# A ring of eleven 2 MB weight blocks over the mixer's buffers, and 32 experts written out, in a one-layer decoder kernel in fp32

## The reference, cut to what matters

```python
h = rmsnorm(x, norm_mix_g)
x = x + hybrid_mixer(h, w_in, conv_w, w_gk_up, b_gk_up, gla_norm_g, w_out)
h = rmsnorm(x, norm_ffn_g)
x = x + moe(h, w_router, b_router, w_gate_up, b_gate_up, w_down, b_down)
out = rmsnorm(x, norm_final_g)

def moe(h, ...):
    top_v, top_i = lax.top_k(h @ w_router + b_router, 4)    # 32 logits for each token
    gates = softmax(top_v)
    # for each expert e, over the tokens that chose it:
    gu = xb @ w_gate_up[e] + b_gate_up[e]                   # 1024 -> 2048
    gate, up = min(gu[:, :F], 7), clip(gu[:, F:], -7, 7)
    y += gate_e * (((up + 1) * gate * sigmoid(1.702 * gate)) @ w_down[e] + b_down[e])   # 1024 -> 1024
```

## Time and profile before

| | |
|---|---|
| time, median of 3 runs | 1104.35 us (1102.31 to 1104.95) |
| the profiled execution's own time | 1101.66 us |
| its span in the trace | 1099.9 us |
| TensorE busy | 1021.7 us, 93% of the span |
| VectorE busy | 222.4 us, 20% |
| ScalarE busy | 163.9 us, 15% |
| read from HBM | 422.56 MB, 385 GB/s over the span |
| mean granted TensorE clock | 0.991 |

### The profile page before, as it was taken

One profiled execution on the slowest core, in us unless ns is written; L12 is line 12 of the kernel. 1 busy time (PEld: TensorE's weight loads), 2 busy tenths in 40 slices (PEclk: granted clock), 3 DMA queues, 4 the chain that ended last, 5 costly groups with the idle time before them and its releaser, 6 DMA issues.

```text
span 1099.9 us, 12562 instructions
## 1 busy us (share of the span) xinstructions
PE 1021.7 (93%) x4660; PEld 393.9 (36%) x4660; DVE 222.4 (20%) x621; ACT 163.9 (15%) x316; POOL 9.6 (1%) x25
## 2 busy tenths in 40 slices
PE   6999989999999999999999999999999999999995
PEld 5588553333333323333333333333332333233331
DVE  1253141111111111111111111111111111111113
ACT  2211021111111111111111111111111111111112
POOL 2000000000000000000000000000000000000000
PEclk9999979999999999999999999999999999999998
DMA  9823338999999999999999999999999999999994
GB/s 375 320 86 144 105 153 343 430 428 429 429 429 429 429 428 428 428 427 429 428 428 428 428 427 429 429 429 428 428 429 429 429 429 428 428 428 427 429 428 170
DMA packets 31337, 423.77 MB, mean 385 GB/s; under 512 B 4623, under 2 KB 4798, under 8 KB 5694
## 3 DMA queue, kind: packets, MB, share of 16 engines
q1 hardware_dynamic: 29454, 421.57, 90.8%
q10 hardware_dynamic: 1872, 2.05, 0.7%
HBM read 422.56 MB, written 1.05 MB: 385 GB/s over the span
## 4 chain that ended last, share of the span: by engine, by line
DMA 59%; PE 38%; DVE 1%; issue 1%; ACT 1%; SPq 0%; ACTq 0%; PEldq 0%; DVEq 0%
DMA ring<-in_w_down 58%; PE bank L1129 13%; PE bank L1116 8%; PE bank L916 6%; PE bank L1005 3%; PE bank L1145 2%; PE bank L912 1%; PE bank L1070 1%; PE bank L1178 1%; DMA x_sb<-in_x 0%; PE bank L1024 0%; PE bank L904 0%; PE bank L1078 0%; DVE y_out L875 0%; PE bank L977 0%
## 5 line engine op out<-in xcount | busy, mean ns | idle before, releaser
L1116 PE MATMUL bank<-ring,x_t 128*64 128x512 f32 x2048 | 466.4, 598 | 13.5 <-DMA ring<-in_w_gate_up 12.5
L1129 PE MATMUL bank<-ring,act 128*64 128x512 f32 x1024 | 239.0, 598 | 32.3 <-DMA ring<-in_w_down 32.3
L1116 PEld LDWEIGHTS bank<-ring,x_t 128*64 128x64 f32 x2048 | 134.0, 136 | 295.7 <-issue 244.1
L1129 PEld LDWEIGHTS bank<-ring,act 128*64 128x64 f32 x1024 | 68.5, 136 | 173.8 <-issue 117.7
L824 DVE TENSOR_TENSOR gu_b<-bank,bias_e 128x512 f32<-128x512 f32 x64 | 44.2, 691 | 350.8 <-PE bank L1145 350.8
L768 DVE TENSOR_SCALAR p_row<-slot,rank 128x64 f32 (+1 forms) x64 | 13.3, 252 | 394.4 <-issue 394.3
L533 ACT COPY gu_sb<-bank 128x512 f32<-128x512 f32 x64 | 37.4, 585 | 244.0 <-PE bank L1116 244.0
L916 PE MATMUL bank<-h_t,ring 128*128 128x256 f32 x320 | 70.3, 380 | 1.3 <-ACT h_t L425 1.3
L1178 PE MATMUL bank<-z,p_t 64*128 64x512 f32 x256 | 63.6, 615 | 0.7 <-ACT z L549 0.7
L916 PEld LDWEIGHTS bank<-h_t,ring 128*128 128x128 f32 x320 | 60.4, 190 | 10.0 <-ACT h_t L425 1.5
L1070 PE MATMUL bank<-h,p_row 128*64 128x512 f32 x256 | 62.2, 607 | 0.0
(11 more groups left out here) (184 smaller groups left out, 334.5 us busy)
## 6 DMA issues: line engine op xcount, KB each, us to landing
ring<-in_w_gate_up SPq DMA_DIRECT2D x128, 2048.0 KB, 24.0
ring<-in_w_down SPq DMA_DIRECT2D x64, 2048.0 KB, 24.4
ring<-in_w_in SPq DMA_DIRECT2D x6, 2048.0 KB, 20.2
ring<-in_w_out SPq DMA_DIRECT2D x2, 2048.0 KB, 11.7
x_sb<-in_x SPq DMA_DIRECT2D x2, 512.0 KB, 4.1
out<-y_out SPq DMA_DIRECT2D x2, 512.0 KB, 2.7
gffn_bc<-in_norm_ffn_g ACTq DMA_DIRECT2D x1, 512.0 KB, 11.0
g_bc<-in_norm_final_g ACTq DMA_DIRECT2D x1, 512.0 KB, 26.3
```

Source lines behind the costliest of these rows:

```text
L1116: ins = mm(bank[h][a * SLOTS:(a + 1) * SLOTS, :], x_t[:, k, :], w[:, kk, a, :], start=k == 0, stop=k == KT - 1)
L1129: ins = mm(bank[0][a * SLOTS:(a + 1) * SLOTS, :], act[:, k, :], w[:, kk, a, :], start=k == 0, stop=k == KT - 1)
```

## The change

- `ring` has eleven slots of 2 MB in place of six. All SBUF tensors get addresses by hand. Slots 6 to 10 lie over the mixer's temporaries (`slot_at(6)` to `slot_at(10)`), so each can be loaded for an expert only when the mixer has done with what lies there.
- SP's first eleven expert loads wait for different things: four for mixer chunks as before, number 4 for the decays and the turned k, 5 to 7 for the attention's and convolution's outputs, 8 and 9 for the two `w_out` chunks, 10 for the gates; from number 11 on a load waits for the use of the chunk that is eleven before it.
- The 32 experts are written out on PE, ACT, DVE and SP, with no loop; further items, where there are any, run one by one in a loop of their own behind them (`If(n > E)`).
- `h2` is gone: `p_row` holds the norm factor in place of ones, the gather takes x itself, and the norm's weights are multiplied in when DVE (no longer ACT) keeps the turned rows as `x_t` (`keep_turned`).
- The first gather stands ahead of the sums for the table; the table's sums and the `b_down` products (now four of fp32 with 32 rows each, no split copy) stand in item 0, behind its first chunk (`start_sums`).
- Small parameters come in one array of columns (`cols_in`), `w_router` and `b_gate_up` are laid out on the host as they are used, so two small turns and the sixteen of L1043 go. `b_gate_up` and `b_down` are loaded early on ACT's queue; `norm_final_g` at the end, on SP's queue, into a slot that is free by then.

The core of the diff:

```diff
-RING = 6
+RING = 11
+MIX_SLOTS = 6
+ORDER = (2, 3, 4, 5, 6, 7, 8, 9, 0, 1, 10)
+LOADED_BEFORE = (2, 2, 1, 1, 1, 1, 0, 0, 0, 0, 0)
+LAST = (E - 1) * ITEM_CHUNKS
...
+def expert_slot(it, j):
+    g = it * ITEM_CHUNKS + j if isinstance(it, int) else LAST + j
+    return ORDER[g % RING]
...
+        ring = [at(f"ring{i}", [P, CHUNK], slot_at(i)) for i in range(RING)]
...
 @block.sync
-            with sp.Fori(0, E) as it:
-                load_item(it, it)
+            for it in range(E):
+                for j in range(ITEM_CHUNKS):
+                    g = it * ITEM_CHUNKS + j
+                    if g < 4:
+                        sp.wait_ge(s_used, 2 + g + 1)
+                    elif g == 4:
+                        sp.wait_ge(s_dec, 4)
+                        sp.wait_ge(s_ex, 3)
+                        sp.wait_ge(s_kt, 1)
+                    elif g == 5:
+                        sp.wait_ge(s_o, 2)
+                        sp.wait_ge(s_ms, 2)
+                        sp.wait_ge(s_ygla, 2)
+                    elif g == 6:
+                        sp.wait_ge(s_o, 2)
+                    elif g == 7:
+                        sp.wait_ge(s_ygla, 2)
+                        sp.wait_ge(s_yconv, 2)
+                    elif g < 10:
+                        sp.wait_ge(s_used, MIX_CHUNKS)
+                    elif g == 10:
+                        sp.wait_ge(s_gtk, 1)
+                    else:
+                        sp.wait_ge(s_used, MIX_CHUNKS + g - RING + 1)
+                    load(it, j, it)
...
 @block.vector
-                dve.scalar_tensor_tensor(out=h2[:, t, :], in0=xs[:, t, :], scalar=rstd[:, t:t + 1],
-                                         in1=gffn_bc[:, :], op0=ALU.mult, op1=ALU.mult).then_inc(s_h2, 1)
...
-                    dve.tensor_scalar(p_row[:, t, :], s1[:, ds(boff, SLOTS)], rank1[:, t, ds(e, 1)], None, ALU.is_equal)
+                    dve.tensor_scalar(p_row[:, t, :], slots, rank1[:, t, ds(e, 1)], rstd[:, t:t + 1],
+                                      ALU.is_equal, ALU.mult)
...
+            def keep_turned(it):
+                dve.wait_ge(s_xT, it + 1)
+                g = cols[:, COL_FFN:COL_FFN + KT].rearrange("p (a f s) -> p a f s", a=2, s=1)
+                dve.tensor_tensor(x_t[:, :, :].rearrange("p (a f) s -> p a f s", a=2),
+                                  bank[3][:, :].rearrange("p (f a s) -> p a f s", f=4, a=2),
+                                  g.broadcast_to([P, 2, 4, SLOTS]), ALU.mult).then_inc(s_xt, 1)
...
 @block.tensor
+            def start_sums():
+                pe.wait_ge(s_hot, 1)
+                for a in range(2):
+                    for b in range(nb):
+                        ins = mm(bank[7][0:1, 128 + a * EXTRA:128 + (a + 1) * EXTRA],
+                                 exp_c[:, 0:1] if a == 0 else boff_c[:, b:b + 1], hot[:, b, :],
+                                 start=b == 0, stop=b == nb - 1)
+                ins.then_inc(s_tab, 1)
+                pe.wait_ge(s_gtk, 3)
+                pe.wait_ge(s_bias, 16 * (1 + SPLITS))
+                pe.wait_ge(s_table, 1)
+                for t in range(TT):
+                    for nn in range(2):
+                        i = 2 * t + nn
+                        ins = mm(y_ps[t][nn][:, :], gates_t[i * E:(i + 1) * E, t, :], bdn[i * E:(i + 1) * E, :],
+                                 start=True, stop=True, tile_position=(i * E, 0))
+                ins.then_inc(s_mixed, 1)
...
-            with pe.Fori(0, final) as it:
-                products(it, last=False)
-            products(final, last=True)
+            for it in range(E):
+                if it == 2:
+                    pe.wait_ge(s_items, 1)
+                    n = pe.value_load(n_items[0:1, 0:1], min_val=E, max_val=E + EXTRA)
+                products(it, it + 1 if it + 1 < E else None)
+            with pe.If(n > E):
+                with pe.Fori(E, n) as it:
+                    pe.wait_ge(s_p, it + 1)
+                    pe.wait_ge(s_ptk, it)
+                    gather()
+                    turn_gathered(it)
+                    products(it, None)
```

More of the change, by code:

```diff
@@ L44, with mix_slot, expert_loaded, build @@
 HALF = 512
[L47 to L52, removed]
+ORDER = (2, 3, 4, 5, 6, 7, 8, 9, 0, 1, 10)
+LOADED_BEFORE = (2, 2, 1, 1, 1, 1, 0, 0, 0, 0, 0)
+LAST = (E - 1) * ITEM_CHUNKS
+SPARE = [ORDER[(LAST + ITEM_CHUNKS + j) % RING] for j in range(RING - ITEM_CHUNKS)]
+LOW = 16928
+KEPT = 32192
+assert LOW + KEPT + RING * SLOT_BYTES <= 229344
+def mix_slot(m):
+    return m % MIX_SLOTS
+def expert_slot(it, j):
+    g = it * ITEM_CHUNKS + j if isinstance(it, int) else LAST + j
+    return ORDER[g % RING]
+def expert_loaded(it, j):
+    g = it * ITEM_CHUNKS + j if isinstance(it, int) else LAST + j
+    n = LOADED_BEFORE[ORDER[g % RING]] + g // RING + 1
+    return 16 * n if isinstance(it, int) else (it + (n - (E - 1))) * 16
+def build(nc, x, cols_in, w_in, w_gk_down, w_gk_up, w_out, w_router, b_router, w_gate_up, b_gate_up, w_down, b_down, norm_final_g, out):
     f32 = mybir.dt.float32
@@ new lines, in at, with row, slot_at @@
+        def at(name, shape, offset, dt=f32):
+            return nc.alloc_sbuf_tensor_at(name, shape, dt, offset=LOW + offset)
+        def row(names, offset, limit):
+            made = []
+            for name, shape, dt in names:
+                made.append(at(name, shape, offset, dt))
+                offset += -(-4 * int(np.prod(shape[1:])) // 32) * 32
+            assert offset <= limit, (names[0][0], offset, limit)
+            return made
+        def slot_at(i):
+            return KEPT + i * SLOT_BYTES
@@ new lines, in build @@
+        ring = [at(f"ring{i}", [P, CHUNK], slot_at(i)) for i in range(RING)]
+        xs = at("x_sb", [P, TT, D], 0)
+        y_t = at("y_t", [P, KT, T], 8192)
+        gu_sb, x_t, p_row, p_gate = row((("gu_sb", [P, 2, HALF], f32), ("x_t", [P, KT, SLOTS], f32),
+                                         ("p_row", [P, TT, SLOTS], f32), ("p_gate", [P, TT, P], f32)), 8192, 16384)
+        x_row = at("x_row", [P, HALF], 8192)
+        z = at("z", [P, HALF], 8192 + 2048)
+        gates4 = at("gates4", [P, TT, SPLITS, E], 8192 + 2048)
@@ L932, in _ @@
             pe.wait_ge(s_pk, 3)
-            pe.wait_ge(s_cols, 2)
             for a in range(PAIRS):
@@ L1053, in _, with gather, turn_gathered @@
             ins.then_inc(s_cnt, 1)
+            def gather():
+                for t in range(TT):
+                    for a in range(2):
+                        ins = mm(bank[3][a * SLOTS:(a + 1) * SLOTS, :], p_row[:, t, :], xs[:, t, a * HALF:(a + 1) * HALF],
+                                 start=t == 0, stop=t == TT - 1)
+                ins.then_inc(s_xg, 1)
+            def turn_gathered(it):
+                pe.wait_ge(s_xr, it + 1)
+                for f in range(4):
+                    ins = nc.tensor.transpose(bank[3][:, f * P:(f + 1) * P], x_row[:, f * P:(f + 1) * P], ident[:, :])
+                ins.then_inc(s_xT, 1)
+            pe.wait_ge(s_p, 1)
+            gather()
             pe.wait_ge(s_more, 1)
@@ L1170, in products @@
                 down(5, range(4))
-                if not last:
-                    turn_gathered(it + 1)
+                if following is not None:
+                    turn_gathered(following)
                 pe.wait_ge(s_z, it + 1)
```

421 lines of the change are left out of this document (151 added, 270 removed).

## The result

The changed kernel takes 1087.39 us (median of 4 runs, 1085.4 to 1087.49) against 1103.95 for the kernel before (4 runs, 1102.31 to 1104.95): ratio 0.9847, 95% interval 0.983 to 0.9864. It is faster by 1.5%, where the forecast had it slower by 2%. The profiled execution has a span of 1085.6 us, 14.3 less than before.

The account below looks back on a forecast made before the run. Expert loads were taken as the bound: last landing 1058.4 + 45.9 for instruction packets = 1104.3, plus a 17.0 tail gives span 1121.3, about 1126 us on the runs' scale. Range 1109 to 1134, or 1098 to 1134 with half the packet cost.

Parts of the forecast that it names:

- The bound: Whole kernel: the expert loads, not PE, set the pace, at 4.894 us a chunk against PE's 27.17 us an item.
- the slots: Ring of eleven: loads 0 to 10 are in before item 0 starts, so the end comes 24.5 us earlier before fetch costs.
- the tail: After the last landing: product, addition, norm and store stay at 17.0 us.
- The 2.7 us: Added at the end because the profiled execution before was that far under the median of the runs.
- The start: Item 0 begins near 163.7, its chunk 1 is used at 174.8, and load 12 lands at 182.4.
- this low stretch: Item 0 at the low granted clock: up to 3 us more, counted only in the forecast's range.
- One chunk: Saturated loads in the expert loop: each chunk takes 4.894 us, 179 of them following load 12.
- missing microsecond: Kernel before: summed loads end at 1081.8, one short of 1082.9, explained by one instruction packet in the saturated stretch.
- The failed step: Written-out PE items: 31 instruction packets all fall on one DMA engine, 45.9 us in all; chance 0.72.
- The price of a packet: Each PE instruction packet costs the DMA engine that serves it 1.48 us, bounds 0.93 and 1.5 us.
- simplest reading: PE's instruction packets: one queue of one sequencer, packets not split, hence always the same DMA engine; chance 0.72.
- Rival 1: Instruction packets spread over 16 engines or cost nothing: 2.9 us, span 1078.3, 1083 on the runs' scale; chance 0.18.

## Why the prediction was wrong

**The bound, the slots, the tail: right.** The loads set the end before and after; five slots are worth 22 to 27 us by the three ways above (forecast 24.5); loads 0 to 10 went out ahead of item 0; PE's item takes 222.59 - 195.42 = 27.17 us early on; queue 8 has 38 packets (forecast 35 to 40); the tail is 17.1 us (17.0). The 2.7 us that the forecast added for the runs' median were not there: the profiled execution took 1087.49 us, the median is 1087.39.

**The start: 1.3 us short.** Item 0 began at 164.25 (forecast 163.7), and its chunk 0 took 5.35 us and not 3.65, at the lower clock. Chunk 1 was used at about 175.9 (174.8), load 12 landed at 183.72 (182.4). The forecast named this low stretch only as part of its range. From the end of chunk 0's products to chunk 1's, sums and `b_down` products between them, 2.6 us went by and not the 3.4 forecast (the `b_down` products took 1.14, not 2.0), so misses partly cancel here.

**One chunk: 4.903 us, not 4.894.** The forecast's quotient is rounded (2.097 MB at 428 GB/s are 4.900 us), but 4.894 is what a chunk takes in the kernel before: its first DMA engine has 4.894 us a chunk from 231 to 1040 us. The changed kernel's needs (1060.99 - 188.22) / 178 = 4.903 us from load 13 on. Over 179 chunks that is 1.6 us. It is neither the slots nor PE's packets: the kernel before with PE written out has 4.893, and every variant of the changed kernel has 4.903 or 4.904, with six slots, and in loops with hardly a packet. Something else of the change does it; no run shows what.

The "missing microsecond" of the forecast is the packet, as it said: in the kernel before, the landing at 187.10 is the first behind the packet at 181.46, it comes 5.78 us after the last one and not 4.89, and the largest lag goes from 0.7 to 1.6 us there and stays.

**The failed step** is "If PE's packets always come on the same engine, that engine has 48 packets of weights and one of instructions for an item [...] 31 x 1.48 = 45.9 us", with its chance of 0.72. The price of a packet was right: steps of 1.4 to 1.6 us of lag, each time the turn came round to the last engine. The engine was not the same: they take turns over eight, so each pays for every eighth packet, 5.7 us in all. In the profile the last engine's lag grew from 0.9 us at load 12 to 7.5, by 6.6 us in four visits; the first, of 2 us, came by the landing at 191.2.

The sum with these sizes: 1058.4 + 1.3 (start) + 1.6 (chunk) + 0.5 (a gap in the first engine's loads between 12 and 13) + 6.6 (lag, in place of 45.9) = 1068.4, measured 1068.5.

The forecast's seven packets could not tell one engine from eight, and the text said so; "simplest reading" was then given 0.72, when a full factor of eight or sixteen in the largest term hung on it. That each engine has a ring of its own for a queue was taken as speaking for one engine; it says nothing of how many of the rings a stream uses. Rival 1 (spread over the engines, 1083 us) had the right mechanism, and by its sixteen engines 3 us too little. The Trainium skill (Runtime: NRT & Kernel Launch, Instruction fetch mechanics) calls such a fetch mostly hidden; the measured 5.9 us in 1100 for 29 packets agree with "mostly", though not with nothing.

Open: why eight engines and not sixteen, which stream of queue 14 it is that always met the same one, and why a chunk takes 0.009 us longer in the changed kernel.

## What to carry to other kernels

Before a small cost is multiplied by the number of items, ask on which of the parallel servers it falls: a transfer that is complete when the slowest of 16 is done pays the largest share of any of them, not the sum and not the mean. Where DMA is the bound, each engine's own landing of a chunk shows that share directly. Writing loops out isn't free there: a loop whose body stays in the engine's buffer, with as many items to a pass as it takes for the slot numbers to repeat, kept nearly all of the deeper ring. And when PE idles ahead of a stretch that others wait for, look at the granted clock of what comes next.

## What the runs showed of the hardware

- PE's instruction packets (queue 8, 16 KB; in the changed kernel 0.96 to 1.00 us from 70 to 190 us, 1.02 to 1.11 us from 200 to 1050, with the DMA engines full) rotate over eight of the sixteen DMA engines and set one back by 1.4 to 1.6 us each; 29 of them, with PE alone written out, cost 5.9 us.
- Packets of queue 14 (8 KB) carry the instructions of other engines. In the kernel with nine slots and PE's loop, the five of 0.325 us all set back the same DMA engine, by about 1 us each; the three of 0.31 us set back others by about 0.4 us.
- A loop body of 82 KB stays in PE's buffer and one of 180 KB doesn't; then the branch back stalls PE for 4.47 us. The Trainium skill (Runtime: NRT & Kernel Launch, Instruction fetch mechanics) gives PE 128 KiB, between the two, and says that a taken branch stalls on a fetch where its target isn't in the current window of two pages. The rows agree with the size and the stall, but not with two pages of 16 KiB as PE's window: back to the start of a body of 82 KB there is no stall. It also says that kernels prefer full unrolling for this reason; in this kernel, with its short bodies, loops on all engines were the faster form (0.9897 for 0.9946, nine slots).
- The first 64 products took 14.05 to 16.18 us in executions of nearly the same code, by when the granted clock reached its upper level: 2 us that a single profile can't attribute.
